# The first four weight slabs as two pairs in 1024-byte packets, and x's first rows two at a time

## The chip, the cores and the metric

One core of one Trainium2 chip runs the kernel. The metric is the device time of one launch in microseconds (us), lower is better. All times on the trace's axis count from the start of the span.

## The reference, cut to what matters

One inference step of a one-layer decoder trunk (d_model 2048) for 256 prompt tokens and 8 sample tokens that share all weights: 264 token columns. What the change touches is the very first part, the normalized input and the first columns of the input projection:

```python
a = _rmsnorm(h, n_pre_mix)
z = jnp.einsum('bld,dn->bln', a, w_in)
(zq, zf, zi, zg, gq, gk, gv, gr, glr, m_h, m_g) = jnp.split(z, IN_SPLITS, axis=-1)
```

Behind it come the two recurrences, the merge, an output projection, an MLP and a gate, all of them further matmuls against streamed weights in f32 precision.

## The kernel before, in words

All weights lie in HBM as `stream[tile, p, k*128 + c]`: tile `tile` gives 128 output features, `k` runs over 16 blocks of 128 input features, `p` is the input feature inside a block. Precision is kept by splitting each number into a rounded part and its rest. ScalarE (ACT) rounds a loaded slab, `whi` from `raw`; VectorE (DVE) makes the rest, `wlo = raw - whi`; TensorE (PE) multiplies hi by hi, hi by lo and lo by hi. The input `x` is treated alike: ACT makes `a_hi` (with the norm's gain), DVE makes `a_lo`. A slab is 128 x 1024 numbers, 512 KB; there is a ring of RING = 4 slabs.

Most tiles are done one after another, each as two slabs of 4096 bytes a partition. The first eight tiles (`WIDE` = 8, the interleaved stretch, T_RANK = 0) are done side by side in eight PSUM banks: slab k holds block k of all eight tiles, so that the PE can start when one block of x is there. `wide` runs k from 0 to 15; for one k it does the small rank tile with two matmuls and seven tiles with three each, 23 in all (here "k0", "k1" and so on are these slabs). Such a slab is fetched by `load_wide` from eight places, 128 numbers each, so the run that is contiguous in HBM is 512 bytes.

The order of the work around the change:

- SP issues every load on one queue: gains, x's block 0, k0 in two halves of four tiles each, x's block 1, k1 in two halves (`HALVED` = 2), x's blocks 2 and 3 in one, k2, k3, x's blocks 4 to 7, then k4, x's blocks 8 to 11, k5, k6, k7, x's blocks 12 to 15, k8 and so on. The sizes of the pieces of x stand in `X_PARTS`. From k4 on a load first waits until the slab that lay in its ring slot has been split (`lo_ready`, line 346).
- ACT goes through k in order: `a_hi` of block k in three pieces (line 969; the second piece reads its tokens backwards, `MIRROR`), then the rounding of slab k (lines 973 and 975 for the halves of a halved slab, 355 for a whole one), then the square of x's block k for the norm (lines 952, 956).
- DVE goes through k in order: `a_lo` (line 1345), then the rest of the slab in `rank_rest` (lines 366 and 368; line 1353 for the second half of a halved slab).
- PE first does 12 matmuls of ones (line 695), then `wide` (lines 398, 400, 403). It starts a halved slab when its first half is split, and the second four tiles when the second half is.

Of the kernel before, what the change touches and what calls it, by code (L numbers as in the profile page):

```python
# [28 lines left out]
P = 128  # L29
# [8 lines left out]
RANK = 16  # L38
# [9 lines left out]
SLAB = HT * P  # L48
RING = 4


WIDE = 8
FIRST = WIDE // 2
SPARE = TOK // 2
X_PARTS = {0: 1, 1: 1, 2: 2, 4: 4, 8: 4, 12: 4}
HALVED = 2


S_GROUP = 32
# [13 lines left out]
T_RANK = 0  # L73
# [18 lines left out]
F32 = mybir.dt.float32  # L92
F32R = mybir.dt.float32r
ALU = mybir.AluOpType
# [7 lines left out]
def build(nc, t):  # L102
# [5 lines left out]
    def sb(name, shape, dt=F32):  # L108
        return ctx.enter_context(nc.sbuf_tensor(name, shape, dt))

    def sem(name):
        return ctx.enter_context(nc.semaphore(name))


    raw = sb("raw", [P, RING, SLAB])
    whi = sb("whi", [P, RING, SLAB], F32R)
    wlo = sb("wlo", [P, RING, SLAB], F32R)
# [86 lines left out]
    slab_landed = [sem(f"slab_landed{i}") for i in range(RING)]  # L204
    hi_ready = sem("hi_ready")
    lo_ready = sem("lo_ready")
    slabs_multiplied = sem("slabs_multiplied")
    tiles_drained = sem("tiles_drained")

    x_landed = [sem(f"x_landed{i}") for i in range(len(X_PARTS))]  # L210
    const_landed = sem("const_landed")
# [9 lines left out]
    ms_ready, s2_ready, r1_ready = sem("ms_ready"), sem("s2_ready"), sem("r1_ready")  # L221
    norm_sum_ready, root_ready, r_ready = sem("norm_sum_ready"), sem("root_ready"), sem("r_ready")
    gains_landed = sem("gains_landed")
    first_landed = [sem(f"first_landed{k}") for k in range(HALVED)]
    first_hi, first_lo = sem("first_hi"), sem("first_lo")
    gates_ready, gates_stored = sem("gates_ready"), sem("gates_stored")
    silu_done = sem("silu_done")
# [98 lines left out]
    def slot_of(par, half):  # L326
        return 2 * par + half
# [13 lines left out]
    def load_wide(sp, T, k, tile, first=False):  # L341

        par, half = (T + k // 2) % 2, k % 2
        s = slot_of(par, half)
        if not first:
            sp.wait_ge(lo_ready, 2 * T + (k - RING + 1))
        src = t["stream"][tile:tile + WIDE, :, k * P:(k + 1) * P].rearrange("n p c -> p n c")
        sp.dma_start(raw[:, s, :].rearrange("p (n c) -> p n c", n=WIDE), src).then_inc(slab_landed[s], 16)

    def round_slab(act, T, par, half, first=False):  # L350
        s = slot_of(par, half)
        act.wait_ge(slab_landed[s], 8 * T + (16 - 8 * par))
        if not first:
            act.wait_ge(slabs_multiplied, 2 * T + (half - RING + 1))
        act.copy(whi[:, s, :], raw[:, s, :]).then_inc(hi_ready, 1)  # L355
# [3 lines left out]
        dve.wait_ge(hi_ready, 2 * T + (half + 1))  # L359
        dve.tensor_tensor(wlo[:, s, :], raw[:, s, :], whi[:, s, :].bitcast(F32), ALU.subtract).then_inc(lo_ready, 1)  # L360

    def rank_rest(dve, T, par, half, end, done):

        s = slot_of(par, half)
        hi = whi[:, s, 0:RANK].bitcast(F32)
        dve.tensor_tensor(whi[:, s, RANK:2 * RANK], raw[:, s, 0:RANK], hi, ALU.subtract)
        at = slice(P, end)
        dve.tensor_tensor(wlo[:, s, at], raw[:, s, at], whi[:, s, at].bitcast(F32), ALU.subtract).then_inc(done, 1)

    def multiply(pe, T, par, half, out, hi, lo, k0, start, stop, before_k=None, midway=None, at=HT // 2):  # L370

# [21 lines left out]
    def wide(pe, T, hi, lo, ready, base, n, free=None, norm=None):  # L393
# [11 lines left out]
        for k in range(KT - 2):  # L405
            pe.wait_ge(ready, base + k + 1)
            if T == T_RANK and k < HALVED:
                pe.wait_ge(first_lo, k + 1)
            else:
                pe.wait_ge(lo_ready, 2 * T + k + 1)  # L410
            for i in range(WIDE):
                if T == T_RANK and k < HALVED and i == FIRST:
                    pe.wait_ge(lo_ready, k + 1)
# [22 lines left out]
    def wide_slab(T, k):  # L436
        return T + k // 2, (T + k // 2) % 2, k % 2
# [7 lines left out]
    def part_of(j):  # L445
        return slice(j * SPARE, (j + 1) * SPARE)

    def part_of_first(half):
        return slice(half * FIRST * P, (half + 1) * FIRST * P)
# [14 lines left out]
    def _(sp):  # L464
        def load_x(i):
            k = list(X_PARTS)[i]
            sp.dma_start(x_in[:, k:k + X_PARTS[k], :], t["x"][:, k:k + X_PARTS[k], :]).then_inc(x_landed[i], 16)

        sp.dma_start(gains[:], t["gains"]).then_inc(gains_landed, 16)
        load_x(0)  # L470
        for k in range(HALVED):
            if k:
                load_x(k)
            for half, landed in enumerate((first_landed[k], slab_landed[k])):
                at = T_RANK + FIRST * half
                sp.dma_start(raw[:, k, part_of_first(half)].rearrange("p (n c) -> p n c", n=FIRST),
                             t["stream"][at:at + FIRST, :, k * P:(k + 1) * P].rearrange("n p c -> p n c")).then_inc(landed, 16)
        load_x(2)
        load_wide(sp, T_RANK, 2, T_RANK, first=True)
        load_wide(sp, T_RANK, 3, T_RANK, first=True)  # L480
        load_x(3)
        for k in range(RING, KT - 4):
            load_wide(sp, T_RANK, k, T_RANK)
            if k in (RING, RING + 3):
                load_x(4 + (k - RING) // 3)
        for dst, name in ((masks, "masks"), (ident, "ident"), (head_gain, "head_gain"),
                          (gate_b, "gate_b")):
            sp.dma_start(dst[:], t[name]).then_inc(const_landed, 16)
# [147 lines left out]
        for u in range(N_RING):  # L636
            T = N_FF + WIDE + 2 + 2 * u
# [299 lines left out]
    def _(act):  # L937
# [9 lines left out]
        def square(n, k, src):  # L947

            if k == 0:
                if n:  # L950
                    act.wait_ge(norm_sum_ready, n)
                act.activation(sq[:, 1, :], src, ACT.Square).then_inc(summed[n], 1)
                return
            if k > 2:
                act.wait_ge(summed[n], k - 1)
            act.activation(squares[:, k % 2, :], src, ACT.Square).then_inc(act_squared[n], 1)
# [8 lines left out]
        for k in range(KT):  # L965
            if k in X_PARTS:
                act.wait_ge(x_landed[list(X_PARTS).index(k)], 16)
            for to, of in MIRROR:
                last = act.activation(a_hi[:, k, to], x_in[:, k, of], ACT.Identity, scale=gains[:, 0, k:k + 1])
            last.then_inc(a_hi_ready, 1)  # L970
            if k < HALVED:
                act.wait_ge(first_landed[k], 16)
                act.copy(whi[:, k, part_of_first(0)], raw[:, k, part_of_first(0)]).then_inc(first_hi, 1)
                act.wait_ge(slab_landed[k], 16)
                act.copy(whi[:, k, part_of_first(1)], raw[:, k, part_of_first(1)]).then_inc(hi_ready, 1)
            else:
                round_slab(act, *wide_slab(T_RANK, k), first=k < RING)
            square(0, k, x_in[:, k, :])
        act.wait_ge(consts_set, 1)
        act.activation(warm[:], eps_col[:], ACT.Sqrt)  # L980
# [346 lines left out]
    def _(dve):  # L1327
# [14 lines left out]
        for k in range(KT):  # L1342
            dve.wait_ge(a_hi_ready, k + 1)
            for to, of in MIRROR:
                last = dve.scalar_tensor_tensor(out=a_lo[:, k, to], in0=x_in[:, k, of], scalar=gains[:, 0, k:k + 1],
                                                in1=a_hi[:, k, to].bitcast(F32), op0=ALU.mult, op1=ALU.subtract)
            last.then_inc(a_lo_ready, 1)
            if k < HALVED:
                dve.wait_ge(first_hi, k + 1)
                rank_rest(dve, *wide_slab(T_RANK, k), FIRST * P, first_lo)  # L1350
                at = part_of_first(1)
                dve.wait_ge(hi_ready, k + 1)
                dve.tensor_tensor(wlo[:, k, at], raw[:, k, at], whi[:, k, at].bitcast(F32), ALU.subtract)\
                   .then_inc(lo_ready, 1)
            else:
                dve.wait_ge(hi_ready, 2 * T_RANK + k + 1)
                rank_rest(dve, *wide_slab(T_RANK, k), SLAB, lo_ready)
        for k in range(KT, KT + 2):
            rest_slab(dve, *wide_slab(T_RANK, k))

# [111 lines left out]
        for n in range(V_TILES):  # L1472
            T = T_V + n
# [269 lines left out]
        for j in range(2):  # L1743
            at = part_of(j)
# [27 lines left out]
        for j in range(FF_BLOCKS):  # L1772
# [18 lines left out]
            if j == 0:  # L1791
# [29 lines left out]
                T = T0 + WIDE + 1  # L1821
# [7 lines left out]
                for i in range(4):  # L1829
                    T = T0 + WIDE + 2 + i  # L1830
# [10 lines left out]
            for n in range(KT):  # L1841
                T = T0 + KT + n
# [220 lines left out]
```

## Time and profile before

| | us |
|---|---|
| three runs, median (lowest to highest) | 1628.49 (1628.38 to 1629.86) |
| the profiled execution | 1628.97 |
| its span on the core | 1627.2 |
| PE busy in the span | 1620.3 |
| DVE, ACT busy | 1109.9, 842.2 |

The profiled execution took 1.8 us more than its span, for what lies around it. TensorE is busy from end to end. The DMA engines moved 202 GB/s on average over the span; between 6 and 24 us, in the stretch that fetches in 512-byte runs, they moved 285 to 353 GB/s.

### The profile page before, as it was taken

How to read it: one execution, taken by the hardware profiler on the slowest of the kernel's cores; microseconds unless marked ns; L12 is line 12 of the kernel's file. 1: busy time of each engine (PE TensorE's matmuls, PEld its weight loads, DVE VectorE, ACT ScalarE, POOL GpSimd, SP SyncE). 2: the span in 40 equal slices, each digit the busy share in tenths (PEclk: the TensorE clock that was granted, in tenths of full speed). 3: DMA queues.
4: the chain of work that ended last, by engine and by line, in shares of the span. 5: the costliest groups of instructions: out<-in, count | busy, mean ns of one | idle time of the engine just before them, and what ended most of it. 6: DMA issues, size and time to landing. Idle time of an engine off the chain costs nothing.

```text
span 1627.2 us, 35049 instructions
## 1 busy us (share of the span) xinstructions
PE 1620.3 (100%) x13332; PEld 1615.8 (99%) x13332; DVE 1109.9 (68%) x1917; ACT 842.2 (52%) x1192; POOL 181.7 (11%) x166
## 2 busy tenths in 40 slices
PE   9999999999999999999999999999999999999999
PEld 9999999999999999999999999999999999999999
DVE  7548767888888876655986665566555665555774
ACT  7575765666666665433654334443444334443452
POOL 3101000111111100055300000000000000035200
PEclk9999999999999999999999999999999999999999
DMA  9577895565555467755675865588557775555564
GB/s 274 161 230 225 267 270 174 164 191 162 192 166 181 155 206 229 270 181 185 173 214 186 247 207 180 188 259 243 174 181 242 245 222 185 181 197 181 167 192 144
DMA packets 151178, 329.17 MB, mean 202 GB/s; under 512 B 16944, under 2 KB 79536, under 8 KB 150608
## 3 DMA queue, kind: packets, MB, share of 16 engines
q1 hardware_dynamic: 143888, 326.00, 64.3%
q10 hardware_dynamic: 7232, 2.43, 0.6%
q8 instruction: 33, 0.54, 0.1%
q14 instruction: 25, 0.20, 0.0%
HBM read 310.08 MB, written 18.30 MB: 202 GB/s over the span
## 4 chain that ended last, share of the span: by engine, by line
PE 98%; DMA 1%; DVE 1%; ACT 0%; SPq 0%; issue 0%
PE bank L380 29%; PE bank L381 29%; PE bank L382 28%; PE bank L398 3%; PE bank L400 3%; PE bank L403 2%; PE bank L768 1%; DMA raw<-in_stream 1%; PE bank L795 0%; PE bank L787 0%; PE bank L766 0%; PE bank L788 0%; PE bank L757 0%; PE bank L732 0%; PE bank L770 0%; PE bank L778 0%
## 5 line engine op out<-in xcount | busy, mean ns | idle before, releaser
L355 ACT CAST whi<-raw 128x1024 fp32r<-128x1024 f32 x532 | 547.9, 1048 | 470.7 <-PE bank L382 388.5
L380 PE MATMUL bank<-a_hi,whi 128*128 128x264 f32 x2576 | 734.2, 285 | 0.1
L381 PE MATMUL bank<-a_hi,wlo 128*128 128x264 f32 x2576 | 729.7, 283 | 0.0
L382 PE MATMUL bank<-a_lo,whi 128*128 128x264 f32 x2576 | 729.4, 283 | 0.0
L360 DVE TENSOR_TENSOR wlo<-raw,whi 128x1024 fp32r<-128x1024 f32 x518 | 629.6, 1246 | 109.8 <-ACT whi L355 108.8
L380 PEld LDWEIGHTS bank<-a_hi,whi 128*128 128x128 f32 x2576 | 485.2, 188 | 0.8 <-issue 0.7
L381 PEld LDWEIGHTS bank<-a_hi,wlo 128*128 128x128 f32 x2576 | 485.5, 188 | 0.1
L382 PEld LDWEIGHTS bank<-a_lo,whi 128*128 128x128 f32 x2576 | 482.9, 187 | 0.0
L380 PE MATMUL bank<-b_hi,whi 128*128 128x264 f32 x1280 | 363.1, 284 | 0.0
L381 PE MATMUL bank<-b_hi,wlo 128*128 128x264 f32 x1280 | 362.6, 283 | 0.0
L382 PE MATMUL bank<-b_lo,whi 128*128 128x264 f32 x1280 | 362.4, 283 | 0.0
L381 PEld LDWEIGHTS bank<-b_hi,wlo 128*128 128x128 f32 x1280 | 241.2, 188 | 0.0
L380 PEld LDWEIGHTS bank<-b_hi,whi 128*128 128x128 f32 x1280 | 241.1, 188 | 0.0
L382 PEld LDWEIGHTS bank<-b_lo,whi 128*128 128x128 f32 x1280 | 239.9, 187 | 0.0
L1281 ACT ACTIVATE lev<-lev 128x264 f32<-128x264 f32 x64 | 27.2, 425 | 165.5 <-DVE lev L1777 165.5
L1690 DVE TENSOR_TENSOR room<-room,bank 128x264 f32<-128x264 f32 (+1 forms) x48 | 20.6, 429 | 106.9 <-PE bank L382 106.9
L1883 POOL TENSOR_TENSOR sq<-room 128x264 f32<-128x264 f32 x2 | 2.2, 1086 | 721.9 <-DVE room L1690 620.0
L398 PE MATMUL bank<-b_hi,whi 128*128 128x264 f32 x256 | 73.3, 286 | 0.3 <-DVE b_lo L1339 0.3
L403 PE MATMUL bank<-b_hi,wlo 128*128 128x264 f32 x256 | 72.8, 284 | 0.0
L400 PE MATMUL bank<-b_lo,whi 128*128 128x264 f32 x256 | 72.7, 284 | 0.0
L1783 DVE TENSOR_TENSOR a_lo<-lev,a_hi 128x264 f32 (+1 forms) x64 | 27.3, 432 | 63.8 <-ACT a_hi L1283 63.8
L1777 DVE SCALAR_TENSOR_TENSOR lev<-bank,r_bc 128x264 f32<-128x264 f32 x64 | 27.1, 432 | 52.6 <-PE bank L382 52.5
(222 smaller groups left out, 1497.7 us busy)
## 6 DMA issues: line engine op xcount, KB each, us to landing
raw<-in_stream SPq DMA_DIRECT2D x532, 512.0 KB, 4.7
m_spill<-stage SPq DMA_DIRECT2D x32, 132.0 KB, 3.7
lev<-m_spill SPq DMA_DIRECT2D x16, 264.0 KB, 2.8
room<-in_x SPq DMA_DIRECT2D x7, 528.0 KB, 7.8
S<-in_state_hgrn SPq DMA_DIRECT2D x6, 512.0 KB, 6.7
out_new_hgrn_sample<-S SPq DMA_DIRECT2D x6, 512.0 KB, 6.8
S<-in_state_gla SPq DMA_DIRECT2D x5, 512.0 KB, 6.7
out_new_gla_sample<-S SPq DMA_DIRECT2D x5, 512.0 KB, 7.5
```

The source lines that it names most:

```text
L355: act.copy(whi[:, s, :], raw[:, s, :]).then_inc(hi_ready, 1)
L360: dve.tensor_tensor(wlo[:, s, :], raw[:, s, :], whi[:, s, :].bitcast(F32), ALU.subtract).then_inc(lo_ready, 1)
L380: pe.matmul(out, whi[:, s, w], hi[:, k0 + k, :], start=start and k == 0, stop=False)
L381: pe.matmul(out, wlo[:, s, w], hi[:, k0 + k, :], start=False, stop=False)
L382: mm = pe.matmul(out, whi[:, s, w], lo[:, k0 + k, :], start=False, stop=stop and k == HT - 1)
L398: pe.matmul(out, whi[:, s, w], hi[:, k, :], start=k == 0, stop=False, skip_group_check=True)
L400: mm = pe.matmul(out, whi[:, s, w], lo[:, k, :], start=False, stop=rank and k == KT - 1, skip_group_check=True)
L403: return pe.matmul(out, wlo[:, s, w], hi[:, k, :], start=False, stop=k == KT - 1, skip_group_check=True)
L1281: act.activation(u, u, ACT.Square).then_inc(u_ready, 1)
L1690: ins = dve.tensor_tensor(out, out, MM[par][:, 0:TOK], ALU.add)
L1777: dve.scalar_tensor_tensor(out=u, in0=bank[:, 0:TOK], scalar=0.0, in1=r_bc[:], op0=ALU.max, op1=ALU.mult).then_inc(tiles_drained, 1)
L1783: dve.tensor_tensor(a_lo[:, T - T0, :], u, a_hi[:, T - T0, :].bitcast(F32), ALU.subtract).then_inc(a_lo_ready, 1)
```

## The change

The slabs k0 to k3 are no longer fetched one by one. `load_pair(k)` fetches blocks k and k+1 together, again in two halves of four tiles: each of its two DMAs moves 512 KB in contiguous runs of 1024 bytes, and writes one of two neighbouring ring slots, in which the blocks k and k+1 alternate. `paired(k)` is the view on the pair that picks block k of all eight tiles: rows of 128 numbers that lie 256 numbers apart. ACT and DVE read `raw` through it for k below 4; `whi` and `wlo` stay dense.

Only k0 is still rounded and split in two halves (`HALVED` = 1). x comes as blocks 0 and 1, then 2 and 3, then as before. The loads of k4 and k5 both wait for k1's split, those of k6 and k7 for k3's, since a pair's two slots are free only when both of its blocks are read. ACT waits for both halves of the second pair before k2.

```diff
-X_PARTS = {0: 1, 1: 1, 2: 2, 4: 4, 8: 4, 12: 4}
-HALVED = 2
+X_PARTS = {0: 2, 2: 2, 4: 4, 8: 4, 12: 4}
+HALVED = 1
...
-            sp.wait_ge(lo_ready, 2 * T + (k - RING + 1))
+            sp.wait_ge(lo_ready, 2 * T + (k - RING + (2 if T == T_RANK and k in (RING, RING + 2) else 1)))
...
+    def paired(k):
+        return raw[:, k // 2 * 2:k // 2 * 2 + 2, :].rearrange("p s (n b c) -> p (s n) b c", n=FIRST, b=2)[:, :, k % 2, :]
...
+        def load_pair(k):
+            for half in range(2):
                 at = T_RANK + FIRST * half
+                sp.dma_start(raw[:, k + half, :].rearrange("p (n c) -> p n c", n=FIRST),
+                             t["stream"][at:at + FIRST, :, k * P:(k + 2) * P].rearrange("n p c -> p n c")).then_inc(slab_landed[k + half], 16)
+        load_pair(0)
+        load_x(1)
+        load_pair(2)
         load_x(2)
-        load_wide(sp, T_RANK, 2, T_RANK, first=True)
-        load_wide(sp, T_RANK, 3, T_RANK, first=True)
-        load_x(3)
...
             if k < HALVED:
-                act.wait_ge(first_landed[k], 16)
-                act.copy(whi[:, k, part_of_first(0)], raw[:, k, part_of_first(0)]).then_inc(first_hi, 1)
-                act.wait_ge(slab_landed[k], 16)
-                act.copy(whi[:, k, part_of_first(1)], raw[:, k, part_of_first(1)]).then_inc(hi_ready, 1)
+                act.wait_ge(slab_landed[0], 16)
+                act.copy(by_block(whi[:, k, part_of_first(0)]), paired(k)[:, 0:FIRST, :]).then_inc(first_hi, 1)
+                act.wait_ge(slab_landed[1], 16)
+                act.copy(by_block(whi[:, k, part_of_first(1)]), paired(k)[:, FIRST:WIDE, :]).then_inc(hi_ready, 1)
+            elif k < RING:
+                if k == 2:
+                    act.wait_ge(slab_landed[2], 16)
+                    act.wait_ge(slab_landed[3], 16)
+                act.copy(by_block(whi[:, k, :]), paired(k)).then_inc(hi_ready, 1)
             else:
-                round_slab(act, *wide_slab(T_RANK, k), first=k < RING)
+                round_slab(act, *wide_slab(T_RANK, k))
```

DVE's `rank_rest` and its second half of k0 read `paired(k)` in the same way.

## Rows read from the trace of the kernel before

**Rows 1.** The page's first line.

```profile
span 1627.2 us, 35049 instructions
```

**Rows 2.** Waits of the PE, whole span: total us, times, longest us.

```profile
PE bank L398 <- DVE wlo L368: 1.1, 2, 0.9
PE bank L398 <- DVE b_lo L1339: 0.3, 1, 0.3
```

**Rows 3.** Timeline of the PE: start, duration, what; in brackets the idle time before.

```profile
7.21 0.42 PE L398 MATMUL bank<-a_hi,whi 128*128 128x264 f32 x1
...
14.01 0.36 PE L398 MATMUL bank<-a_hi,whi 128*128 128x264 f32 x1 [0.91 <-DVE wlo L368]
...
22.49 0.28 PE L403 MATMUL bank<-a_hi,wlo 128*128 128x264 f32 x1
23.00 0.36 PE L398 MATMUL bank<-a_hi,whi 128*128 128x264 f32 x1 [0.23 <-DVE wlo L368]
```

**Rows 4.** The chain that ended last, first 25 us: start, duration, what.

```profile
11.63 8.94 DMA raw<-in_stream
```

**Rows 5.** Timeline of ACT, first 14 us.

```profile
4.84 0.88 ACT L969 ACTIVATE a_hi<-room,gains 128x128 fp32r<-128x128 f32 x3 [1.46 <-DMA room<-in_x]
...
6.33 0.62 ACT L975 CAST whi<-raw 128x512 fp32r<-128x512 f32 x1
...
7.18 0.87 ACT L969 ACTIVATE a_hi<-room,gains 128x128 fp32r<-128x128 f32 x3
...
9.84 0.89 ACT L969 ACTIVATE a_hi<-room,gains 128x128 fp32r<-128x128 f32 x3 [0.29 <-DMA room<-in_x]
11.61 1.05 ACT L355 CAST whi<-raw 128x1024 fp32r<-128x1024 f32 x1 [0.88 <-DMA raw<-in_stream]
...
12.88 0.87 ACT L969 ACTIVATE a_hi<-room,gains 128x128 fp32r<-128x128 f32 x3
13.66 1.03 ACT L355 CAST whi<-raw 128x1024 fp32r<-128x1024 f32 x1
```

**Rows 6.** Timeline of SP's queue: start of issue, duration, what.

```profile
1.65 0.98 SPq L476 DMA_DIRECT2D raw<-in_stream  x2
...
3.23 0.98 SPq L476 DMA_DIRECT2D raw<-in_stream  x2
...
9.76 0.43 SPq L348 DMA_DIRECT2D raw<-in_stream  x1
```

**Rows 7.** Issue to landing of single DMAs, issued at 1.65, 2.13, 3.7, 27.96 us.

```profile
raw<-in_stream SPq DMA_DIRECT2D x1, 256.0 KB, 3.9
...
raw<-in_stream SPq DMA_DIRECT2D x1, 256.0 KB, 4.2
...
raw<-in_stream SPq DMA_DIRECT2D x1, 256.0 KB, 4.9
...
raw<-in_stream SPq DMA_DIRECT2D x1, 512.0 KB, 4.4
```

**Rows 8.** DMA of 24.5-27, 42-44, 15.2-16.2 us: packets, MB, share of 16 engines.

```profile
q1 hardware_dynamic: 1283, 0.64, 99.0%
...
q1 hardware_dynamic: 129, 0.48, 84.5%
...
DMA packets 191, 0.38 MB, mean 380 GB/s; under 512 B 7, under 2 KB 114, under 8 KB 191
...
q1 hardware_dynamic: 191, 0.38, 103.2%
```

**Rows 9.** Timeline of DVE, the rest of slab k2.

```profile
12.78 1.08 DVE L368 TENSOR_TENSOR wlo<-raw,whi 128x896 fp32r<-128x896 f32 x1
```

**Rows 10.** Line 969, first 45 us: shortest, median, longest ns; first, last start.

```profile
L969 ACT ACTIVATE a_hi<-room,gains x48: 283/386/403, 4.8 to 42.7; 128x128 fp32r<-128x128 f32 x32, 128x8 fp32r<-128x8 f32 x16
```

**Rows 11.** Lines 695 and 703, fp32 matmuls early and late: the same columns.

```profile
L695 PE MATMUL bank<-ones x24: 421/421/553, 1.7 to 6.7; 128*128 128x128 f32 x24
...
L703 PE MATMUL bank<-rank_z,gate_w x8: 381/381/485, 60.6 to 62.3; 32*128 32x264 f32 x8
```

More of the change, by code:

```diff
@@ L223, in build @@
     gains_landed = sem("gains_landed")
-    first_landed = [sem(f"first_landed{k}") for k in range(HALVED)]
     first_hi, first_lo = sem("first_hi"), sem("first_lo")
@@ L360, in rest_slab, with by_block, rank_rest @@
         dve.tensor_tensor(wlo[:, s, :], raw[:, s, :], whi[:, s, :].bitcast(F32), ALU.subtract).then_inc(lo_ready, 1)
-    def rank_rest(dve, T, par, half, end, done):
+    def paired(k):
+        return raw[:, k // 2 * 2:k // 2 * 2 + 2, :].rearrange("p s (n b c) -> p (s n) b c", n=FIRST, b=2)[:, :, k % 2, :]
+    def by_block(ap):
+        return ap.rearrange("p (n c) -> p n c", c=P)
+    def rank_rest(dve, T, par, half, end, done, rows=None):
         s = slot_of(par, half)
+        rows = by_block(raw[:, s, :]) if rows is None else rows
         hi = whi[:, s, 0:RANK].bitcast(F32)
-        dve.tensor_tensor(whi[:, s, RANK:2 * RANK], raw[:, s, 0:RANK], hi, ALU.subtract)
+        dve.tensor_tensor(whi[:, s, RANK:2 * RANK], rows[:, 0, 0:RANK], hi, ALU.subtract)
         at = slice(P, end)
-        dve.tensor_tensor(wlo[:, s, at], raw[:, s, at], whi[:, s, at].bitcast(F32), ALU.subtract).then_inc(done, 1)
+        dve.tensor_tensor(by_block(wlo[:, s, at]), rows[:, 1:end // P, :], by_block(whi[:, s, at].bitcast(F32)), ALU.subtract)\
+           .then_inc(done, 1)
     def multiply(pe, T, par, half, out, hi, lo, k0, start, stop, before_k=None, midway=None, at=HT // 2):
@@ L470, in _ @@
         load_x(0)
[L471 to L474, printed above, removed]
+        def load_pair(k):
+            for half in range(2):
                 at = T_RANK + FIRST * half
-                sp.dma_start(raw[:, k, part_of_first(half)].rearrange("p (n c) -> p n c", n=FIRST),
-                             t["stream"][at:at + FIRST, :, k * P:(k + 1) * P].rearrange("n p c -> p n c")).then_inc(landed, 16)
+                sp.dma_start(raw[:, k + half, :].rearrange("p (n c) -> p n c", n=FIRST),
[3 more added lines that the diff above has]
+        load_pair(2)
         load_x(2)
-        load_wide(sp, T_RANK, 2, T_RANK, first=True)
-        load_wide(sp, T_RANK, 3, T_RANK, first=True)
-        load_x(3)
         for k in range(RING, KT - 4):
@@ L484, in _ @@
             if k in (RING, RING + 3):
-                load_x(4 + (k - RING) // 3)
+                load_x(3 + (k - RING) // 3)
         for dst, name in ((masks, "masks"), (ident, "ident"), (head_gain, "head_gain"),
@@ L1349, in _ @@
                 dve.wait_ge(first_hi, k + 1)
-                rank_rest(dve, *wide_slab(T_RANK, k), FIRST * P, first_lo)
+                rank_rest(dve, *wide_slab(T_RANK, k), FIRST * P, first_lo, rows=paired(k))
                 at = part_of_first(1)
                 dve.wait_ge(hi_ready, k + 1)
-                dve.tensor_tensor(wlo[:, k, at], raw[:, k, at], whi[:, k, at].bitcast(F32), ALU.subtract)\
+                dve.tensor_tensor(by_block(wlo[:, k, at]), paired(k)[:, FIRST:WIDE, :], by_block(whi[:, k, at].bitcast(F32)), ALU.subtract)\
                    .then_inc(lo_ready, 1)
@@ L1356, in _ @@
                 dve.wait_ge(hi_ready, 2 * T_RANK + k + 1)
-                rank_rest(dve, *wide_slab(T_RANK, k), SLAB, lo_ready)
+                rank_rest(dve, *wide_slab(T_RANK, k), SLAB, lo_ready, rows=paired(k) if k < RING else None)
         for k in range(KT, KT + 2):
```

## The prediction

> **What bounds the kernel now.** I read the page first, then the PE's waits, then the PE's timeline in the first 25 us, then the chain that ended last, then ACT, SP's queue and the DMAs. The page gives a span of 1627.2 us [rows 1]. The list of what the PE waited for is short: twice for a slab's split in the interleaved stretch, 1.1 us in sum, and once 0.3 us much later [rows 2]. So the PE sets the time, and the change, which moves no matmul, can act only through the moment from which the PE runs without a gap. That moment is early. The PE starts k0 at 7.21, waits for k2 until 14.01, and waits once more for k5 until 23.00, though k4's last matmul began at 22.49 [rows 3]. Those 69 matmuls follow at (22.49 - 14.01) / 68 = 0.125, so k2 to k4 took 8.60 us, 2.87 us a slab, and k5 came 0.39 us late. The last wait decides: without a gap, a k2 start at 23.00 - 8.60 = **14.40** would have given the same end. Whoever lets the PE start k2 by then, with nothing late behind it, loses nothing; each us later costs one us.
>
> What ends the last wait is the load of k5: issued at 11.63, it needs 8.94 us [rows 4], against 4.4 for the same bytes when little lies ahead of them (below). So in this stretch the loads queue, and bytes and packets count.
>
> **The change part by part.** The sum is an arrival time for k2, compared with 14.40.
>
> *x's first two blocks at once.* Block 0 landed at 4.84 [rows 5], which released ACT's first a_hi. Now 132 KB more come with it. The 264 KB of blocks 2 and 3 took from 1.24 us, k1's second half landing at 3.7 + 4.9 = 8.60 [rows 6, 7] and they at 9.84 [rows 5]; half of it is 0.62. At the 380 GB/s of a stretch full of x's long packets [rows 8] it is 0.36. So 5.20 to 5.45; I take 5.3.
>
> *The first pair.* Before, 256 KB took 0.78 us (1.65 + 3.9 = 5.55 for k0's first half, 2.13 + 4.2 = 6.33 for its second [rows 6, 7]), so 1.56 per 512 KB; later, 512 KB of k2 took 11.61 - 9.84 = 1.77 [rows 5]. Packets of 1024 bytes don't stand in the trace, so I bound them. A 512-byte packet took 0.99 x 16 x 2.5 us / 1283 = 30.9 ns. Of the 191 packets of the third stretch, 77 are x's of 4224 bytes; 1.032 x 16 us less 107 x 30.9 ns gives 171 ns each. A straight line puts 1024 bytes at 50 ns against 62 for two of 512: 0.81 of the time. The 116 large packets of the second stretch took 0.845 x 32 us / 116 = 233 ns, and that line gives 60, or 0.97 [rows 8]. I take the middle, 0.89, as nothing tells which stretch is nearer. The two halves of the pair then take 1.39 us each: the first lands at 6.7, the second at T = 5.3 + 2.78 = **8.1** (7.7 with all low ends; 8.6 with 5.45 and no gain from the packets).
>
> The Trainium skill (DMA: Bandwidth & Descriptors, Why small descriptors are slow) puts a fixed cost of about 3 cycles on each packet beside one per 32 bytes; as an estimate 35 cycles against 2 x 19, or 0.92. By that T would be 8.2. The rows allow it, but their line has a larger fixed part, and no run yet shows 1024 bytes.
>
> *k0.* Before, the PE began it at 7.21. Now its first half lands at 6.7, after 5.55, so it starts about a us later. That costs nothing as long as k0 is through before k1 is split. Even with the whole slab's 2.40 us from cast to PE (11.61 to 14.01 [rows 3, 5]) for a half, the second half is ready at 10.5, and its 12 matmuls end at 12.0; k1 comes later, as follows.
>
> *k1 as a whole slab behind k0's second half.* This is what I expect to bind. k1's data lie in the same two DMAs, so both its halves wait for T, and ACT takes k0 first: half cast and square 0.85 (6.33 to 7.18), a_hi of block 1 0.78 (12.88 to 13.66), then k1's cast, and 2.40 from there to the PE [rows 3, 5]; the DVE's 1.08 for the rest is in it [rows 9]. k1 starts at T + 4.03 = 12.1, ends 2.87 later: k2 can start at T + 6.90 = **15.0**, 0.6 after 14.40.
>
> *k2 and k3.* They need both halves of the second pair. x's blocks 2 and 3 land at 8.1 + 1.24 = 9.3, the pair 2 x 1.77 x 0.89 = 3.15 later, at 12.5, against 11.61 for k2 before; ready at 12.5 + 2.40 = 14.9. That is just under the PE's own 15.0.
>
> *Strided rows.* ACT and DVE read rows of 128 numbers with a gap. The trace has no such read. The nearest is line 969, where half of the 128-wide pieces run backwards: median 386 ns, longest 403 [rows 10], 4% apart. I take nothing; at 4% the chain of k1 grows by 0.1.
>
> *The longer wait before k4 to k7.* SP waits until k1 is split (about T + 3.9 = 12.0) before it issues k4, against 9.76 [rows 6]. Queued behind it are x's blocks 8 to 11, k5 and all later loads. With little ahead of it, k4 needs the 4.4 us of a late load [rows 7]: landed at 16.4, ready 18.8; the PE comes to it at 15.0 + 5.74 = 20.7. k5 lies behind 528 KB of x (2 x 1.24 at most) and its own 1.77: landed by 20.65, against 20.57 before [rows 4], ready by 23.05; the PE comes at 23.6. So the PE's own delay hides it, with 0.55 us to spare; past that it costs one for one. k6 is issued when k3 is split, at about 16.8, some 4 us before k5 has landed, so the queue stays fed.
>
> **Sum.** k2 at 15.0 instead of 14.40: +0.6 us on the profiled span (1627.2 to 1627.8). That execution is 1628.97, 0.5 above the median of the runs shown; on the median, 1628.49 + 0.6 = **1629.1**. From the bounds of packets and x alone: T of 7.7 gives +0.2; T of 8.6 and a second pair without gain (8.6 + 1.24 + 3.54 + 2.40 = 15.8) gives +1.4. About 0.2%, 3.3 us, is what a measurement here can tell from no change; all of this lies inside.
>
> **The rivals.**
>
> *Faster loads win.* If the first pair lands at 7.2, k2 starts at 14.1, k5 lands earlier too, and the wait for it is gone: -0.3, 1628.2. For it: x's block 1 as a DMA of its own cost more than its bytes (768 KB and it took 5.55 to 8.60, 3.05 us, of which 2.34 for the slabs at 1.56), and that goes. Against it: even the low ends give 7.7. More than -1.45 can't come: 46 matmuls at 0.125 from 7.21 end at 12.95.
>
> *1024 bytes are no quicker than twice 512.* Then the change doesn't do what it says, and only its coarser grain is left: +1.1 to +1.4, about 1629.8.
>
> *The clock rises later.* Warm-up matmuls of 128 columns took 421 ns, later ones of 264 columns 381 [rows 11], so the start ran at the lower of TensorE's two levels; k0's run at 0.42 and then 0.28. Now the PE stands idle between the warm-up's end (about 7.1) and 8.1, just there. If it stays at the lower level until t, k0 and k1 end at t/2 + 9.8; as long again as 1.7 to 7.2 makes t 13.6 and +2.2, 1630.7. Against it: after the 0.91 us gap before 14.01 the matmuls go on at full pace [rows 3].
> The Trainium skill (TensorE: Matmul & The Clock Gate, Part 1) says that the throttled state is the default and activity releases it. The slow warm-up agrees; whether this idle us is enough, no run here shows.
>
> *Strided rows at half speed (the slower side).* Place: ACT's casts and DVE's rests of k0 to k3. With a factor f, k3 reaches the PE at 8.1 + 3.03 + 2.7 f + 0.15 + 2.25 f, to be held against 14.40 + 2.87: f = 2 gives +3.9, 1632.4. It beats the k1 chain from f = 1.33 and passes 0.2% at f = 1.87. Against it: the 4% above.
>
> **How the numbers follow.** k1's chain binds, +0.2 to +1.1: 0.60. Faster loads, -0.4 to +0.2: 0.16. No gain from packets, +1.1 to +1.8: 0.14. Later clock: 0.07. Strided at half speed: 0.03. The time is that of the first. The range runs from 1627.9, the faster loads with 0.2 for the scatter of a median, to 1630.7, the late clock; it leaves out the strided case and the edges of the others. Faster by over 0.2% has no case but the unknown, 0.01; slower holds the strided case and a long low clock, 0.04; the rest, 0.95, is the same.
>
> **What would show it.** The first matmul of `wide` at about 8; a PE wait of about 1 us before k1; k1's cast on ACT at 9.7; k2 at about 15.0, and no PE wait before k5. Packets of 1024 bytes at 50 to 60 ns. SP held before k4 until 12. Wrong it would be if the PE still waits at k5, if the casts and rests of k0 to k3 are longer than those of k4, or if matmuls of k0 and k1 follow at 0.24.

## The result: 2.0 us slower, 0.13%

| us | median | lowest to highest | runs |
|---|---|---|---|
| before | 1628.48 | 1627.89 to 1630.26 | 21 |
| changed | 1630.48 | 1629.01 to 1631.79 | 21 |

The ratio is 1.0013, with a 95% interval of 1.0007 to 1.0019. So the change costs about 2 us, inside the 0.2% that was called "the same", and more than the 0.6 us of the forecast. The changed runs also scatter more. The profiled executions are 1628.97 before and 1630.21 after, 1.24 apart; the first was half a us above its kernel's median.

### The profile page after: what moved, and what is told of

Read it like the earlier page. It is cut to its first block, busy times and chain, and to the rows that moved or that the text cites. A ratio compares the mean times of both kernels' runs of the same rounds, so it can differ in the third digit from the quotient of the medians.

```text
span 1628.4 us, 35045 instructions
## 1 busy us (share of the span) xinstructions
PE 1620.6 (100%) x13332; PEld 1616.5 (99%) x13332; DVE 1110.7 (68%) x1916; ACT 843.2 (52%) x1191; POOL 183.7 (11%) x166
## 4 chain that ended last, share of the span: by engine, by line
PE 99%; DVE 1%; DMA 0%; ACT 0%; SPq 0%; issue 0%
PE bank L388 29%; PE bank L389 29%; PE bank L390 28%; PE bank L406 3%; PE bank L408 3%; PE bank L411 3%; PE bank L777 1%; PE bank L804 0%; PE bank L796 0%; PE bank L775 0%; DMA raw<-in_stream 0%; PE bank L797 0%; PE bank L766 0%; PE bank L741 0%; PE bank L779 0%; PE bank L787 0%
```

## The profile after

The page's first lines, and the PE's waits over the whole span:

```profile
span 1628.4 us, 35045 instructions
...
PE 1620.6 (100%) x13332; PEld 1616.5 (99%) x13332; DVE 1110.7 (68%) x1916; ACT 843.2 (52%) x1191; POOL 183.7 (11%) x166
```

```profile
PE bank L406 <- DVE wlo L375: 2.2, 1, 2.2
PE bank L704 <- POOL eps_col L1889: 1.7, 1, 1.7
PE bank L406 <- DVE b_lo L1353: 0.3, 1, 0.3
```

Against [rows 2] the two waits for slabs k2 and k5 (1.1 us) have gone, and one of 2.2 us ahead of the first matmul has come. The PE's timeline (line 406 of the changed kernel is line 398 of before; the first rows are k0, then the starts of k1, k2 and k5):

```profile
8.70 0.36 PE L406 MATMUL bank<-a_hi,whi 128*128 128x264 f32 x1 [2.16 <-DVE wlo L375]
...
9.34 0.42 PE L411 MATMUL bank<-a_hi,wlo 128*128 128x264 f32 x1
9.56 0.42 PE L406 MATMUL bank<-a_hi,whi 128*128 128x264 f32 x1
...
13.10 0.28 PE L406 MATMUL bank<-a_hi,whi 128*128 128x264 f32 x1
...
15.91 0.28 PE L406 MATMUL bank<-a_hi,whi 128*128 128x264 f32 x1
...
24.32 0.28 PE L406 MATMUL bank<-a_hi,whi 128*128 128x264 f32 x1
```

k2 starts at 15.91 and k5 at 24.32, against 14.01 and 23.00 [rows 3]: k5 is 1.32 later, and the span 1.2. That is the whole difference between these two profiles: from k5's start to the end of the span it is 1604.2 us before and 1604.1 after. In all fourteen profiles of this study that time is 1604.0 to 1604.9, so what happens in the first 24 us is carried to the end, to within 0.9 us.

ACT in the same stretch (line 978 makes a_hi; 982 and 984 round k0's halves, 989 rounds k1 and then k2):

```profile
5.88 0.89 ACT L978 ACTIVATE a_hi<-room,gains 128x128 fp32r<-128x128 f32 x3 [2.40 <-DMA room<-in_x]
7.26 0.62 ACT L982 CAST whi<-raw 128x512 fp32r<-128x512 f32 x1 [0.49 <-DMA raw<-in_stream]
8.64 0.62 ACT L984 CAST whi<-raw 128x512 fp32r<-128x512 f32 x1 [0.76 <-DMA raw<-in_stream]
...
10.27 1.03 ACT L989 CAST whi<-raw 128x1024 fp32r<-128x1024 f32 x1
...
12.30 1.04 ACT L989 CAST whi<-raw 128x1024 fp32r<-128x1024 f32 x1
```

and the DVE's rest of k1:

```profile
11.42 1.09 DVE L375 TENSOR_TENSOR wlo<-raw,whi 128x896 fp32r<-128x896 f32 x1
```

x's first two blocks release ACT at 5.88, where block 0 alone came at 4.84 [rows 5]. The two halves of the pair are 1.38 apart, the second is cast at T = 8.64. From there the forecast chain runs as written: k1's cast 1.63 later, its split done at 11.42 + 1.09 = 12.51, ready for the PE near 12.65, T + 4.0. But the PE is not there: it is still at k0, at 0.22 us a matmul. The stretches show why (columns: stretch and length, busy us of PE, its weight load, DVE, ACT and GpSimd, granted clock, DMA share, GB/s):

```profile
8.00:10.00 2.00, 1.30 (x8) 1.33 (x9) 1.25 (x3) 1.36 (x4) 0.00 (x0) 0.79 1.09 379
10.00:12.00 2.00, 2.00 (x11) 2.00 (x11) 1.42 (x5) 2.00 (x6) 0.30 (x1) 0.50 0.77 288
12.00:14.00 2.00, 2.00 (x16) 2.00 (x16) 2.00 (x6) 2.00 (x6) 1.39 (x2) 0.86 0.12 33
```

The granted clock goes to 0.50, the lower of TensorE's two levels, for a while after the 2.16 us of idling, and is back before 14. k1 therefore starts at 13.10, 0.45 after it was ready.

The loads. DMA packets from 4.0 to 5.0 us, nearly all of 1024 bytes, and those from 11.0 to 12.0:

```profile
DMA packets 346, 0.34 MB, mean 341 GB/s; under 512 B 13, under 2 KB 346, under 8 KB 346
...
q1 hardware_dynamic: 346, 0.34, 97.1%
...
DMA packets 70, 0.19 MB, mean 186 GB/s; under 512 B 13, under 2 KB 30, under 8 KB 70
...
q1 hardware_dynamic: 70, 0.19, 47.0%
```

A 1024-byte packet takes 0.971 x 16 us / 333 = 47 ns, against 2 x 30.9 [rows 8]: 0.75 of the time. But those 30.9 ns come from 24.5 to 27 us. From 9 to 10 us the kernel before moved packets of 512 bytes almost alone:

```profile
DMA packets 667, 0.34 MB, mean 343 GB/s; under 512 B 6, under 2 KB 664, under 8 KB 667
...
q1 hardware_dynamic: 667, 0.34, 114.4%
```

There one took 1.144 x 16 us / 661 = 27.7 ns, which makes the ratio 0.84, and the bytes moved as fast as in the first stretch above, 343 GB/s against 341. So a pair's packets take 0.75 to 0.84 of the time, and the rate of the transfer is not shown to be higher.

In the stretch from 11 to 12 us the engines are less than half busy, yet 17 packets of 1024 bytes are still under way, 0.8 us at 47 ns: about what one engine does in that time, while the others seem to be through with the pairs. The first pair looks alike. From 6 to 7 us, 75 packets of over 2 KB are begun, which are of x's blocks 2 and 3 and stand behind that pair in the queue, though its second half is there only at 8.64:

```profile
DMA packets 272, 0.34 MB, mean 341 GB/s; under 512 B 19, under 2 KB 197, under 8 KB 272
```

ACT waits for a load's whole count of 16, so engines that are out of step keep the saved packet time from being seen.

SP's queue shows the wait for a pair's slots; k4's load is issued at 12.54 (9.76 before [rows 6]), and the stretch from 12 to 14 above has 33 GB/s:

```profile
12.54 0.37 SPq L347 DMA_DIRECT2D raw<-in_stream  x1
```

It costs nothing: the PE does not wait for k4 to k7.

Strided rows, by form in the first 24 us (line 989 reads with gaps, 354 dense; the last column but one is the mean ns of one):

```profile
L375 DVE TENSOR_TENSOR wlo<-raw,whi 128x896 fp32r<-128x896 f32 x5 | 5.4, 1082 | 0.0
...
L354 ACT CAST whi<-raw 128x1024 fp32r<-128x1024 f32 x3 | 3.2, 1055 | 2.1 <-DMA raw<-in_stream 2.1
L989 ACT CAST whi<-raw 128x1024 fp32r<-128x1024 f32 x3 | 3.1, 1035 | 0.0
```

## The experiments

Each ran on the chip beside the kernel before. At most 1 us separates many of these medians, and their intervals overlap; so a verdict rests on the profile as well as on the time.

**1. A longer warm-up on the changed kernel (after_warm20).**

```diff
-        for _ in range(12):
+        for _ in range(20):
             pe.matmul(DG[:, 0:P], ones[:], ones[:], start=True, stop=True)
```

> The changed kernel with 20 instead of 12 warm-up matmuls of ones, so that the PE is busy until k0's first half is split at about 8.7 us; nothing else moves. Theory (late first loads plus a low clock): the change costs 1.1 us through k1's split at 12.7 us, and the rest of its 2.0 us is the lower clock that the PE's idle time ahead of 8.7 us brings. Then k0's matmuls follow at 0.12 us, k2 starts at about 15.5, and the time is 1629.4 to 1629.8, with less scatter than the changed kernel's 1629.0 to 1631.8. Rival (loads alone): the clock only fills time in which the PE would wait anyway, and the time stays at 1630.5. Second rival: the extra warm-up matmuls run at the lower level and push k0 back; then k0 starts after 9.5 and the time is 1630.5 or more.

Measured: 1630.31 (1629.39 to 1635.66), ratio 1.0014 (1.0005 to 1.0023). The theory failed here: with the clock at full level from 6.1 us on, the time hardly moves. ACT's cast of k0's second half, and the PE's waits for that half and for k1:

```profile
9.51 0.62 ACT L984 CAST whi<-raw 128x512 fp32r<-128x512 f32 x1 [3.09 <-DMA raw<-in_stream]
```

```profile
10.91 0.39 PE L406 MATMUL bank<-a_hi,whi 128*128 128x264 f32 x1 [1.10 <-DVE wlo L1367]
...
13.52 0.36 PE L406 MATMUL bank<-a_hi,whi 128*128 128x264 f32 x1 [0.89 <-DVE wlo L375]
```

k1 starts at T + 4.0 again, with T = 9.51, and now the PE does wait. So the lower clock mostly fills time that k1's chain would cost anyway; T is what counts, and T moves from run to run.

**2. A shorter warm-up on the kernel before (before_warm4):** 4 instead of 12 in the same line.

> The kernel before with 4 instead of 12 warm-up matmuls, so that the PE idles from about 3.5 to 7.2 us; loads, ACT and DVE stay. Clock theory: k0 and k1 run at 0.22 us a matmul until 10.9 to 14 us, k2 starts at 14.8 to 16.3 instead of an equivalent of 14.40, and the time is 0.4 to 1.9 us above the kernel before. Rival (the clock does not matter, the loads set k2 and k5): no difference, within 0.2 us.

Measured: 1628.54 (1627.85 to 1633.07), ratio 1.0003 (0.9994 to 1.0012). Also a miss for the theory, though the lower level is there:

```profile
6.60 0.56 PE L398 MATMUL bank<-a_hi,whi 128*128 128x264 f32 x1 [2.86 <-DVE wlo L368]
6.95 0.42 PE L400 MATMUL bank<-a_lo,whi 128*128 128x264 f32 x1
7.17 0.42 PE L398 MATMUL bank<-a_hi,whi 128*128 128x264 f32 x1
```

k0 started at 6.60 and not at 7.2; from there the lower clock can last until about 9.9 before it costs anything: by then half of 3.3 us of work is done, and the other 5.74 - 1.65 us of k0 and k1 end at 14.0, when k2 arrives. In this profile it lasted longer and k2 began at 14.96; over the runs it cost nothing that shows.

**3. x's block 0 alone again (after_x1).**

```diff
-X_PARTS = {0: 2, 2: 2, 4: 4, 8: 4, 12: 4}
+X_PARTS = {0: 1, 1: 1, 2: 2, 4: 4, 8: 4, 12: 4}
...
         load_pair(0)
         load_x(1)
+        load_x(2)
         load_pair(2)
-        load_x(2)
+        load_x(3)
```

> The changed kernel, but x's blocks 0 and 1 come in two loads again: block 0 first, then the first pair, then block 1, then blocks 2 and 3, then the second pair. Theory: x's block 0 lands at about 4.85 instead of 5.88, the first half of the pair at 6.3 instead of 7.2, the second at 7.7 instead of 8.6, so k1 is split at 11.7 and k2 can start at 14.6. The PE's idle time before k0 falls from 2.2 to about 1 us. Time 1628.7 to 1629.5. Rival (the pairs, not x, make the loss): first half of the pair lands after 7, time 1630 or more.

Measured: 1629.47 (1628.93 to 1631.11), ratio 1.0006 (0.9997 to 1.0016). The pair's second half is cast at 7.29, so k1 starts at 11.30, T + 4.0 for the third time; after it k2 waits a little for the second pair:

```profile
7.29 0.62 ACT L985 CAST whi<-raw 128x512 fp32r<-128x512 f32 x1 [0.75 <-DMA raw<-in_stream]
...
12.11 1.05 ACT L990 CAST whi<-raw 128x1024 fp32r<-128x1024 f32 x1 [1.06 <-DMA raw<-in_stream]
```

```profile
11.30 0.36 PE L406 MATMUL bank<-a_hi,whi 128*128 128x264 f32 x1 [0.89 <-DVE wlo L375]
...
14.52 0.36 PE L406 MATMUL bank<-a_hi,whi 128*128 128x264 f32 x1 [0.17 <-DVE wlo L375]
```

**4. Only x's part of the change (before_x2):** `X_PARTS` as in the change, loads of the slabs as before.

> The kernel before with only the x part of the change: blocks 0 and 1 of x in one load ahead of k0's halves; slabs in 512-byte runs, k0 and k1 halved. Theory: x lands at 5.9 and k0's first half at 6.5, so the PE starts k0 at about 8.3 after 1.1 us of idling, but k2's load, which ends a wait, lands as before at 11.6 and k5's at 20.5: the time moves by 0 to 0.5 us, more only where the clock falls (then k0's matmuls at 0.22 us). Rival (the x part makes most of the loss): 1.0 us or more above the kernel before with the clock at full level.

Measured: 1628.07 (1627.38 to 1628.62), ratio 0.9997 (0.9988 to 1.0006): not slower. Here x's first two blocks were there at 4.25 us and not at 5.9, so the landing of that same load is not a fixed price. The PE's last two waits in this profile are for k2 and k5, as in the kernel before:

```profile
13.10 0.36 PE L398 MATMUL bank<-a_hi,whi 128*128 128x264 f32 x1 [0.33 <-DVE wlo L368]
...
22.34 0.36 PE L398 MATMUL bank<-a_hi,whi 128*128 128x264 f32 x1 [0.47 <-DVE wlo L368]
```

So grouping x costs nothing by itself. That it costs something where all that stands behind it waits for one large first pair is inferred from this and from experiment 3, which had T 1.4 us sooner.

**5. k1 in halves again, on the changed loads (after_halved2).**

```diff
-HALVED = 1
+HALVED = 2
```

> The changed kernel with k1 rounded and split in two halves again, as k0 is; the loads are the changed ones. Theory (k1's whole split behind the second half of the first pair sets k2): from that half's cast at T on, k1's first half reaches the PE at T + 3.1 instead of T + 4.0, so k2 starts 0.6 to 0.9 us sooner (then the second pair, at about T + 6.1, is next) and the time is 1629.5 to 1629.9. Rival (only the later and more scattered first loads count, whatever is done with them): 1630.3 to 1630.5 as before the edit.

Measured: 1629.62 (1627.96 to 1633.14), ratio 1.0009 (1.0000 to 1.0018), 0.9 below the changed kernel's median, and 0.7 when each is held against the kernel before that ran beside it (1.3 against 2.0). T is 8.69 and x's first load as late as in the changed kernel; k1 starts 3.2 after T, without a wait, and not 4.0:

```profile
5.98 0.88 ACT L978 ACTIVATE a_hi<-room,gains 128x128 fp32r<-128x128 f32 x3 [2.51 <-DMA room<-in_x]
...
8.69 0.62 ACT L984 CAST whi<-raw 128x512 fp32r<-128x512 f32 x1 [0.81 <-DMA raw<-in_stream]
```

```profile
11.91 0.36 PE L406 MATMUL bank<-a_hi,whi 128*128 128x264 f32 x1
```

k1 starts at 11.91, k2 at 14.85, k5 at 23.26, against 24.32 with the same loads. Of these 1.06 us, 0.45 belong to the clock, which did not fall in this profile; the other 0.6 are what halving k1 can account for, the lower end of what was expected.

**6. Only the first pair (pair0_only):** k2 and k3 come by `load_wide` again and are read dense.

```diff
-        load_pair(2)
+        load_wide(sp, T_RANK, 2, T_RANK, first=True)
+        load_wide(sp, T_RANK, 3, T_RANK, first=True)
```

> The changed kernel with only the first pair (k0, k1); k2 and k3 come one by one in 512-byte runs and lie dense again. Theory: k1's split behind the first pair binds, so it stays: k2 at T + 6.9, time 1630.1 to 1630.6, as the changed kernel. Rival (the second pair, which k2 needs whole, is the cost): 1628.3 to 1628.8.

Measured: 1629.51 (1628.91 to 1632.79), ratio 1.0007 (0.9998 to 1.0016): below the theory's 1630.1 to 1630.6 and above the rival's. The profiled execution, 1630.75, has the chain once more, from T = 8.90:

```profile
10.30 0.39 PE L406 MATMUL bank<-a_hi,whi 128*128 128x264 f32 x1 [1.56 <-DVE wlo L1365]
...
12.92 0.36 PE L406 MATMUL bank<-a_hi,whi 128*128 128x264 f32 x1 [0.91 <-DVE wlo L375]
```

The mechanism holds. The median is 1 us lower than with both pairs, which suggests that the second pair has a share as well; the intervals overlap, so it is not shown.

**7. Only the second pair (pair2_only):** the kernel before, with k2 and k3 fetched as a pair and read strided; k0, k1 and x as before.

> The kernel before with only the second pair (k2, k3); k0, k1 and x as before. The pair lands whole about 2.8 us behind x's blocks 2 and 3, against 1.8 for k2 alone. Theory: k2 comes to the PE about 1 us later (about 15.0 on the axis of the kernel before), k5 is not waited for any more, so the time rises by 0.4 to 0.9 us: 1628.9 to 1629.4. Rival (the saved packet time pays for it): 1628.0 to 1628.5.

Measured: 1630.82 (1629.41 to 1631.07), ratio 1.0013 (1.0004 to 1.0022), as slow as the whole change and not the expected 1628.9 to 1629.4. The runs lie in two groups: the four whose mean granted clock is 1.0 at 1629.41 to 1630.03, the seven with 0.999 at 1630.67 to 1631.07. The profile is from the first group. k2's cast waits for the whole pair, and the PE for k2:

```profile
12.42 1.04 ACT L991 CAST whi<-raw 128x1024 fp32r<-128x1024 f32 x1 [2.00 <-DMA raw<-in_stream]
```

```profile
14.82 0.36 PE L407 MATMUL bank<-a_hi,whi 128*128 128x264 f32 x1 [2.25 <-DVE wlo L376]
```

k2 is 0.8 later than in [rows 3], as expected. What was not expected is that the idle time of 2.25 us ahead of it costs another 1.5 us in most runs: the medians of the two groups are 1629.46 and 1630.94.

**8. The same with that idle time filled (pair2_fill).**

```diff
+            if T == T_RANK and k == 2:
+                for _ in range(8):
+                    pe.matmul(SC[0][:, TOK:TOK + P], ones[:], ones[:], start=False, stop=False, skip_group_check=True)
             pe.wait_ge(ready, base + k + 1)
```

> The kernel with only the second pair (1630.82, in two clusters, 1629.4 to 1630.0 and 1630.7 to 1631.1), and eight matmuls of ones into unused columns between k1 and k2, about 1.8 of the 2.25 us in which the PE waits there. Clock theory: the upper cluster is the runs whose clock falls after that wait, so it vanishes: all runs at 1629.3 to 1629.8, mean granted clock 1.0 in each. Rival (the second cluster comes from the loads): two clusters as before the edit, median 1630.5 or more. If the added matmuls cost time themselves: one cluster, above 1629.8.

Measured: 1629.26 (1629.05 to 1629.85), ratio 1.0006 (0.9997 to 1.0015), a mean granted clock of 1.0 in all eleven runs. The upper group is gone and the PE has no wait left for a slab:

```profile
PE bank L709 <- POOL eps_col L1894: 1.7, 1, 1.7
PE bank L407 <- DVE b_lo L1358: 0.3, 1, 0.3
```

No load was touched, so it was the clock. What is left, 0.9 us over the kernel before (1628.40 beside it), can be put down to k2's later arrival; the interval of the ratio reaches down to 1.

**9. Both repairs at once (x1_halved2):** the edits of 3 and 5.

> The changed kernel with x's blocks 0 and 1 in two loads and with k1 in halves, the two edits that alone gave 1629.47 and 1629.62. Theory: with both, k1 is no longer the bound, k2's wait for the whole second pair is (cast at about 12.1, PE at 14.5), so little more is gained: 1629.0 to 1629.5. Rival (the gains add, since k1's chain is all that holds the PE): 1628.4 to 1628.8.

Measured: 1629.23 (1628.61 to 1630.46), ratio 1.0004 (0.9995 to 1.0013), as the theory had it: the two gains of about 1 us don't add. ACT's cast of k2 waits for the second pair until 12.19, as expected, which with 2.40 us from cast to PE makes k2 ready at 14.59:

```profile
12.19 1.05 ACT L990 CAST whi<-raw 128x1024 fp32r<-128x1024 f32 x1 [0.37 <-DMA raw<-in_stream]
```

But in this profile the PE does not wait for k2. It idled ahead of k0, ran much of k0 at 0.22 us a matmul (granted clock 0.52 from 8 to 10 us), and came to k2 only at 15.26:

```profile
8.06 0.55 PE L406 MATMUL bank<-a_hi,whi 128*128 128x264 f32 x1 [2.04 <-DVE wlo L375]
...
15.26 0.28 PE L406 MATMUL bank<-a_hi,whi 128*128 128x264 f32 x1
```

The profiled execution (1629.48) is one of the two in eleven whose mean granted clock is 0.999. So the lower clock set k2 here, and that the second pair sets it in the other nine is argued from the cast, not seen.

**10. x's part alone, and x's blocks 8 to 11 behind k5 (x2_x8late).**

```diff
-            if k in (RING, RING + 3):
+            if k in (RING + 1, RING + 4):
```

> The kernel before with x's blocks 0 and 1 in one load (which measured 1628.07), and with x's blocks 8 to 11 and 12 to 15 each issued one slab later, so that k5 no longer lies behind 528 KB of x. Theory: k5's load lands about 1.4 us sooner, the last wait of the PE, 0.5 us, goes, and k2's arrival sets the time: 1627.5 to 1627.8. Rival (k5's wait is hidden or another slab's takes its place): 1628.0 to 1628.2.

Measured: 1628.01 (1627.55 to 1629.08), ratio 0.9998 (0.9989 to 1.0007): no gain over experiment 4. The wait for k5 went, and one for k4 took its place: ACT waited for x's blocks 4 to 7 until 15.35 and then for k4's own load until 16.95.

```profile
16.95 1.05 ACT L355 CAST whi<-raw 128x1024 fp32r<-128x1024 f32 x1 [0.71 <-DMA raw<-in_stream]
```

```profile
13.29 0.36 PE L398 MATMUL bank<-a_hi,whi 128*128 128x264 f32 x1 [0.20 <-DVE wlo L368]
...
19.36 0.36 PE L398 MATMUL bank<-a_hi,whi 128*128 128x264 f32 x1 [0.25 <-DVE wlo L368]
```

No kernel of this study is shown to beat the kernel before.

**11. Second profiles of both kernels (after_again, before_again).**

> The changed kernel once more, for a second profile. Theory: the second half of the first pair is cast at T between 8.0 and 9.5, and k2 starts at T + 6.9 or, where the clock falls or has not risen, later. Rival: k2's start does not follow T.

> The kernel before once more, for a second profile. Theory: its profiled execution of before (1628.97) was 0.5 above its median, so here k5 starts at about 22.5 rather than 23.0, again with a wait for k5's load, and the span is near 1626.7. Rival: k5 at 23.0 again; then the changed kernel lost the rest elsewhere than in the first 25 us.

The changed kernel: 1630.91, T = 8.73, x's first load at 5.97, k1 at 12.97, k2 at 15.91 and k5 at 24.33, the same picture to 0.15 us, the granted clock again at 0.61 between 9 and 13 us. The kernel before: 1629.03, k2 at 13.68 and k5 at 22.28, without a wait for k5; that wait is not in every execution:

```profile
9.50 0.36 PE L398 MATMUL bank<-a_hi,whi 128*128 128x264 f32 x1 [0.43 <-DVE wlo L368]
...
13.68 0.36 PE L398 MATMUL bank<-a_hi,whi 128*128 128x264 f32 x1 [1.14 <-DVE wlo L368]
```

Its span is 1627.2 all the same, as it took 0.7 us more after k5, so the expected 1626.7 was missed.

## Why the prediction was right, and where it was short

- **The range.** 1630.48 lies within 1627.9 to 1630.7, in part by luck. The likeliest case, that k1's chain binds, was priced at +0.2 to +1.1, and the medians are 2.0 apart. The range reached far enough only because its upper end was set by the late clock, and 18 of the changed kernel's 21 runs show no fall of the clock (below).
- **What decides.** Right: only the moment from which the PE runs without a gap counts. From k5's start to the end all profiles agree within 0.9 us.
- **k1's chain.** Right, the likeliest case: k1 is ready at T + 4.03. It reads T + 4.0 in four profiles (12.65 from 8.64, 13.52 from 9.51, 12.92 from 8.90, 11.30 from 7.29), and halving k1 (experiment 5) took 0.7 to 0.9 us off the median.
- **T, the mis-sized term.** 8.1 was forecast, 8.64 and 8.73 came, and 8.69 to 9.51 in the variants that keep x's grouping and the first pair. In both profiles of the changed kernel and in that of experiment 5 the halves' distance, 1.39, was right (1.38 to 1.45), and x's first load came late: 5.88, 5.97 and 5.98, against 5.3. The packet records of these three traces show why: one packet of that load took 1.51, 2.30 and 2.22 us, where the median one took 0.09, and a few of the load's packets came only after it. The same load landed by 4.15 to 4.43 in four other profiles, where no packet of it took over 0.8 us; but two of these then had the pair's second half 3.4 and 3.7 us behind the first, so that T was 8.90 and 9.51 all the same. So the lateness of T is no fixed price of x's size, and it comes with an early x too.
- **The packets.** 0.89 was taken, 0.75 to 0.84 measured, against bounds of 0.81 and 0.97. The Trainium skill's per-packet cost (DMA: Bandwidth & Descriptors, Why small descriptors are slow) would give 0.92; the measurement decides, and the saving is larger. It still didn't show in the landings: all of k0 and k1 was in and being rounded at 8.6 to 9.0 us in the order of before, and at 8.64 to 9.51 in the new one with x's grouping. By then the old order has half of k1 left for ACT and DVE, the new one half of k0 and all of k1.
- **The late clock** was a rival at 0.07, priced by +2.2. Something like it happened in both profiles of the changed kernel, but in a milder form: the clock was up, fell behind the idle time, and cost 0.45 us beyond k1's chain. The idle time ahead of k0 had been taken as 1 us and was 2.16. One of the prediction's own signs of being wrong, matmuls of k0 that follow at 0.24, thus came close to true, at 0.22. But such a fall is the exception: 18 of the changed kernel's 21 runs have a mean granted clock of 1.0, and their median is 1630.47. (That mean shows a fall and not a first rise that is late; it is 1.0 in experiment 2 too.) Experiment 1, which kept the clock up, bounds its part in the median: 0.2 us (1630.48 to 1630.31), less than the intervals can tell. With the second pair alone it was more, 1.5 us in seven runs of eleven. The Trainium skill (TensorE: Matmul & The Clock Gate, Part 1) has a throttled state that lack of activity brings back; experiments 7 and 8 agree.
- **The mark of 14.40.** It came from an execution half a us above its kernel's median. Sum for the profiled pair: 0.6 forecast, + 0.5 for T, + 0.45 for the clock, - 0.25 because k1 to k4 ran 11.22 us and not 2.87 + 8.60; 1.3, and k5 came 1.32 later. The other 0.7 to the medians' 2.0 is that half us, and 0.27 by which the profiled execution of the changed kernel lay below its own.
- **The median run.** No profile shows it. As an estimate from the profiles, with 1.8 us outside the span and 1604.1 from k5 to the end, its k5 starts at 1630.48 - 1.8 - 1604.1 = 24.6, k2 8.4 before that at 16.2, and without a fall of the clock T is 6.9 earlier, about 9.3, give or take the 0.9 us by which the time behind k5 varies. The one profile with these loads and the clock up, that of experiment 1, is near it: T 9.51, k5 at 24.82, 1630.77 us. So T was probably some 1.2 us late in the median, more than the 0.5 of the profiled pair.
- **Strided rows**: 1035 ns against 1055 dense, the DVE's 1082 for all. Nothing, as taken.
- **The later issue of k4**: 12.54 against 12.0 forecast, hidden as forecast.
- **The rival that the packets are no quicker** is out for the single packet by the 47 ns, but the landings came out as it had supposed, no sooner. That faster loads win is out by T.

What stays open: why the first loads land so unevenly. The records show single packets of 1.5 to 2.3 us and packets that trail, not their cause; that one DMA engine lags is read from packet counts alone, and no experiment here moved it on purpose.

## What to carry to other kernels

At the start of a kernel, the size that counts is not that of the packet but of the work that stands behind one landing: a pair of slabs moves its bytes in 0.75 to 0.84 of the packet time, and yet hands them over in one piece, after which the rounding and splitting of a slab and a half lies open where half a slab did. So before making loads coarser, add up what the engines behind them still have to do after the last byte; if it is more than the transfer saves, keep the first pieces small. And look at the idle time of the PE that a coarser load brings: it can cost again through the clock.

## What the runs showed of the hardware

- Idle time of the PE of 2.16 and 2.25 us in the first 15 us was followed by the lower clock level in some executions and not in others: granted clock 0.50 from 10 to 12 us in the profile of the changed kernel, a mean below 1.0 in three of its 21 runs and in seven of eleven runs of experiment 7. Eight matmuls of ones in the gap of experiment 7 removed it in eleven of eleven.
- The same first load of x, 264 KB, was there at 4.15 to 5.98 us in seven profiles, with nothing but 32 KB ahead of it. In the three late ones a single packet of it took 1.51 to 2.30 us, against a median of 0.09.
- Two changes that cost 1.2 and 2.5 us alone (experiments 6 and 7) cost 2.0 together: their costs don't add.
